# Expert gathers with an index bound: rows of empty slots are no longer fetched

## The reference, cut to what matters

```python
def moe_ffn(h, w_rg, b_rg, w_re, b_re, w_g, w_u, w_d):
    ...
    e_idx = grp[:, None] * EXPERTS_PER_GROUP + e_loc
    ...
    xb = h_pad[slot_tok].reshape(n_blk, EXPERT_BLOCK, D)
    ...
    def run(args):
        xe, e = args
        return (jax.nn.silu(xe @ w_g[e]) * (xe @ w_u[e])) @ w_d[e]
    ...
    return jax.ops.segment_sum(y_assign, tok_sorted, num_segments=N).astype(h.dtype)
```

## Time and profile before

| | us |
|---|---|
| median of 3 runs | 993.66 |
| the profiled execution | 996.17 |
| its span, first to last instruction | 994.3 |
| TensorE busy in the span | 948.4 |
| VectorE busy | 550.7 |
| ScalarE busy | 190.1 |
| GpSimd busy | 59.1 |

### The profile page before, as it was taken

How to read it: one execution, slowest core, us unless ns; L and a number is a source line. 1 busy time by engine, 2 the same in 40 slices (tenths; PEclk the granted TensorE clock), 3 DMA queues, 4 the chain that set the end, 5 groups by cost and what they waited for, 6 DMA issues and landing times.

```text
span 994.3 us, 11254 instructions
## 1 busy us (share of the span) xinstructions
PE 948.4 (95%) x4417; PEld 468.3 (47%) x4417; DVE 550.7 (55%) x1074; ACT 190.1 (19%) x419; POOL 59.1 (6%) x70
## 2 busy tenths in 40 slices
PE   5999998999999999889999999999999999998997
PEld 2575666877654445643333333333333333333443
DVE  2205440446876412474777777777776667677133
ACT  4011121002755210131111111111111111112201
POOL 3010023000000000010000000000000000000000
PEclk9999999999999999899999999999999999999899
DMA  9590353250001791559999999999999999999111
GB/s 283 171 304 16 75 156 104 86 189 22 2 1 34 196 412 45 234 218 415 420 421 420 418 420 421 419 419 419 421 419 420 421 418 420 420 421 406 69 42 48
DMA packets 72954, 265.01 MB, mean 267 GB/s; under 512 B 11096, under 2 KB 35044, under 8 KB 47908
## 3 DMA queue, kind: packets, MB, share of 16 engines
q1 hardware_dynamic: 68368, 251.32, 64.5%
q0 software_dynamic: 4080, 12.85, 3.7%
q10 hardware_dynamic: 452, 0.11, 0.1%
HBM read 253.24 MB, written 13.08 MB: 268 GB/s over the span
## 4 chain that ended last, share of the span: by engine, by line
PE 75%; SPq 12%; DMA 6%; DVE 4%; ACT 1%; issue 1%; ACTq 0%; DVEq 0%
PE ps L1002 67%; SPq L348 12%; DMA w<-in_w_exp_up 3%; DMA w<-in_w_exp_down 3%; PE ps L1361 2%; PE ps L1020 1%; PE ps L1618 1%; PE ps L1655 1%; PE ps L1102 1%; PE ps L1103 1%; DVE h L2505 0%; DMA gmix<-in_norm_mix 0%; ACT probs L825 0%; PE ps L1364 0%; PE ps L1170 0%
## 5 line engine op out<-in xcount | busy, mean ns | idle before, releaser
L1002 PE MATMUL ps<-w,xe 128*64 128x512 f32 x1024 | 233.6, 598 | 11.6 <-DMA w<-in_w_exp_up 10.6
L2463 DVE TENSOR_TENSOR h<-h,ps 128x1024 f32<-128x1024 f32 (+1 forms) x150 | 177.4, 1216 | 31.4 <-PE ps L1002 29.4
L1002 PEld LDWEIGHTS ps<-w,xe 128*64 128x64 f32 x1024 | 70.0, 136 | 145.9 <-issue 139.1
L1002 PE MATMUL ps<-w,hT 128*64 128x512 f32 x512 | 116.9, 598 | 0.7 <-DVE hT L2440 0.5
L1002 PE MATMUL ps<-xT,wring 128*128 128x272 f32 x384 | 101.7, 403 | 2.8 <-issue 2.8
L1002 PE MATMUL ps<-yk,ST 128*128 128x512 f32 (+1 forms) x320 | 95.3, 413 | 0.5 <-DVE yk L2454 0.5
L1002 PE MATMUL ps<-wring,xT 128*32 128x128 f32 (+2 forms) x368 | 80.8, 413 | 1.4 <-DVE xT L391 1.4
L1002 PEld LDWEIGHTS ps<-xT,wring 128*128 128x128 f32 x384 | 68.5, 190 | 28.9 <-issue 16.2
L956 ACT ACTIVATE sg<-ps 64x256 f32<-64x256 f32 x64 | 24.1, 377 | 266.5 <-PE ps L1002 266.1
L674 POOL DMA_INDIRECT xg<-hn_rows,sidx x32 | 30.2, 944 | 667.1 <-PE ps L1618 388.3
L1002 PEld LDWEIGHTS ps<-w,hT 128*64 128x64 f32 x512 | 34.4, 136 | 66.6 <-issue 65.8
(11 more groups left out here) (341 smaller groups left out, 867.4 us busy)
## 6 DMA issues: line engine op xcount, KB each, us to landing
w<-in_w_exp_gate SPq DMA_DIRECT2D x64, 1024.0 KB, 26.2
w<-in_w_exp_up SPq DMA_DIRECT2D x64, 1024.0 KB, 27.4
w<-in_w_exp_down SPq DMA_DIRECT2D x64, 1024.0 KB, 27.4
wring<-in_w_in SPq DMA_DIRECT2D x12, 512.0 KB, 6.2
wpg<-in_w_ple_gate SPq DMA_DIRECT2D x2, 2048.0 KB, 13.5
biaslines<-blrow SPq DMA_DIRECT2D x1, 2560.0 KB, 10.6
h<-in_x_prompt SPq DMA_DIRECT2D x4, 512.0 KB, 12.3
wring<-in_w_in SPq DMA_DIRECT2D x2, 1024.0 KB, 10.9
```

Source lines behind the costliest of these rows:

```text
L1002: return nc.tensor.matmul(out, l, r, start=start, stop=stop, skip_group_check=skip)
L2463: TTn(h[0:r, t, :], h[0:r, t, :], both(4 + 2 * (t % 2), r), ALU.add).then_inc(S["hadd"], 1)
```

## The change

Token numbers in `tokf` are lowered by 4096 (`NOROW`), and `2 * 4096` is added when `sidx` is made. A filled slot has the index it had. An empty slot sums to 0 and gets index 8192 or 8193. The gather carries the bound `2 * N - 1 = 1087` and doesn't treat an index over it as an error: such a row is to be left out, and the partition keeps what it held.

```diff
+NOROW = 4096
...
                 pool.indirect_dma_start(out=xg[:, two(J), :], out_offset=None, in_=hn_d.rearrange("n (k d) -> (n k) d", k=2),
-                                        in_offset=bass.IndirectOffsetOnAxis(ap=at, axis=0)).then_inc(S[f"gath{two(J)}"], 16)
+                                        in_offset=bass.IndirectOffsetOnAxis(ap=at, axis=0), bounds_check=2 * N - 1,
+                                        oob_is_err=False).then_inc(S[f"gath{two(J)}"], 16)
...
                     for k in range(2):
-                        V.tensor_copy(tokf[:, k, :], tok[:])
+                        V.tensor_scalar(tokf[:, k, :], tok[:], float(-NOROW), None, ALU.add)
...
-            TS(sidx[0:SLOTS, :], ps[0:SLOTS, 6, 0:JOBS], 2.0, None, ALU.mult)
-            TS(sidx[SLOTS:P, :], ps[0:SLOTS, 6, 0:JOBS], 2.0, 1.0, ALU.mult, ALU.add).then_inc(S["ix_ok"], 1)
+
+            TS(sidx[0:SLOTS, :], ps[0:SLOTS, 6, 0:JOBS], 2.0, 2.0 * NOROW, ALU.mult, ALU.add)
+            TS(sidx[SLOTS:P, :], ps[0:SLOTS, 6, 0:JOBS], 2.0, 2.0 * NOROW + 1.0, ALU.mult, ALU.add).then_inc(S["ix_ok"], 1)
```

## The result

The changed kernel took 985.12 us (median of 4 runs, 984.98 to 987.06), the kernel before 992.95 us beside it (median of 4, 992.14 to 994.12): ratio 0.9923, 95% interval 0.9908 to 0.9938, so 6.2 to 9.1 us less. Forecast was 5.0 us less and 988.7 us; the time lies in the range and the sign is right, the gain is half as large again.

What follows compares the result with a forecast made beforehand. DMA was taken to bound the expert stage, PE waiting for weights after 720 us. The only nonzero term, 5.0 us less for left-out gather rows, took the median 993.66 us to 988.7 us; range 984.0 to 994.7 us.

Steps and rivals of the forecast that it cites:

- The bound: Expert stage: DMA full from about 446 us, PE waiting for weights only after 720 us, at most 11.0 us to gain.
- The steps that cost nothing: VectorE additions, the first two gathers and POOL's index check: each counted as 0 us.
- The layout: Later 30 gathers: each engine writes 4 adjacent partitions and the 4 lying 32 higher; gain 5.0 us within 0 to 9.1.
- the term of the sum: Empty half rows left out of the later 30 gathers, priced at 5.0 us less, between 0 and 9.1 us.
- Rival A: Later gathers: relief is even over the engines, gain 8.7 to 9.1 us, time 984.7 us; chance 0.22.
- rival B: Later gathers: nothing gained, by 8 adjacent slots on the busiest engine or left-out rows costing their packet; 993.7 us, chance 0.22.
- Rival C: First gather: the index check on POOL holds it up, 4 us slower at 997.7 us; chance 0.08.
- Rival D: Expert stage: all of PE's 11.0 us of waits vanish, packets also being cheaper; 982.7 us, chance 0.06.
- the relief that counts is that of the busiest engine: Later gathers: weights land only when all 16 engines finish, so the least relieved counts: 61 half rows at 0.082, 5.0 us.
- what would show it: Signs for the profile after: q0 about 4.2 MB and fewer packets, PE's waits near 6 us, DMA share below 1.01.

Runs made afterwards that it cites:

- e3: Changed kernel with every index over the bound, so no gather fetches a row (timing only); ratio 0.9855 to the kernel before, stage 451.7 us.
- e11: Changed kernel with the bound kept but the indexes of the kernel before, so every row is fetched; ratio 0.9996, stage 464.4 us.
- e12: Changed kernel with the gathers of jobs 0 and 1 fetching all their rows; one run, 990.45 us beside 994.81 us before, stage 457.0 us.
- e1: Changed kernel leaving out slots 32 to 63 in every gather, filled or not (timing only); ratio 0.9886 to the kernel before, stage 455.0 us.
- e2: Changed kernel leaving out slots 4 to 7, 12 to 15 and so on, filled or not (timing only); ratio 0.9997, stage 463.9 us.
- e5: Changed kernel leaving out slots 2, 3, 6, 7 and so on (timing only); one run, 986.27 us beside 995.12 us before, stage 454.9 us.
- e6: Changed kernel fetching only slots 0 to 3 and 32 to 35 (timing only); one run, 991.50 us beside 995.12 us before, stage 460.5 us.
- e8: Changed kernel fetching only slots 28 to 31 and 60 to 63 (timing only); one run, 991.49 us beside 995.12 us before, stage 460.9 us.
- e4: Changed kernel with slots dealt over the engine groups by two constant tables, result kept; 989.42 us beside 995.32 us, ratio 0.9933, stage 456.6 us.
- e9: The changed kernel itself, run and profiled again on another chip; 987.99 us beside 994.81 us before, ratio 0.9925, stage 457.1 us.
- e7: Changed kernel fetching only slots 8 to 11 and 40 to 43 (timing only); one run, 994.05 us beside 995.12 us before, stage 463.4 us.

## Why the prediction was right, and where its size was off

**The bound** was read rightly. PE leads with 14.31 us for a job until the lead of the weight buffers is used up, and bytes left out earlier are paid back only after that. e3 shows that the early ones count: 9 gathers are issued after 720 us (POOL's x9 in the earlier trace rows), which in full cost 9 x 0.66 = 5.9 us, and e3 saved 12.4. The chain now changes at 766 us (forecast about 820), PE's waits are 4.4 us (forecast 6.0).

**The steps that cost nothing** do. The two additions on `tokf` take 168 ns each as the casts of the earlier trace rows did, L2397 and L2398 0.20 us each as in the earlier trace rows. POOL's 53 ns and the first two gathers are settled by e11 and e12.

**The layout** was the point on which the term of the sum hung, between 0 and 9.1 us; e1, e2, e5 and the late increments of e6 to e8 show it as forecast. Rival A fell by e2, although its time, 984.7 us, was nearest to the 985.1 us measured: a right number is not a right mechanism. Of rival B, the form in which a left-out row costs its packet is half there: the number of packets stays, the bytes don't, and 0.06 us of 0.66 us remain for a gather. Rival C fell by e11. Rival D's ceiling is real but not reached; e3 is where it lies.

**The step that failed** is "the relief that counts is that of the busiest engine", which priced the term at 61 x 0.082 = 5.0 us. The runs gave 7.0 us in the stage. The price of a half row was a bit too high (0.076 by e1), so the step by itself would have given only 4.6 us. The main thing is that the fullest group, that of slots 0 to 3, was not the one that set the landings: it has 3.6 us of slack (e6), so it would have allowed 61 x 0.076 + 3.6 = 8.2 us, and the group of slots 8 to 11 would have allowed 100 x 0.076 + 0.7 = 8.3 us. The sum for each engine is its relief plus its slack, and the smallest of these decides. Slots 4 to 7 have the next smallest relief, 87: 6.6 us, which with 0.4 us of slack would be the 7.0 measured. The remaining groups are rid of 111 or more, 8.4 us. The group of slots 4 to 7 was not looked at alone, so which one decides is argued, not shown. What the trace does show is that it is a single engine: in a load of the changed kernel that ends at 877.74 us the last increment comes 0.9 us after the one before it, where in the kernel before the last eight come within 0.7 us (887.95 to 888.58 us).

The rule is good to about half a microsecond. For e4 it gives 100 x 0.076 + 0.4 = 8.0 us for slots 4 to 7, and 7.5 were measured. It also finds an engine with next to no slack: e2 gained 0.2 us with the groups of slots 0, 8, 16 and 24 full, of which the first two have 3.6 and 0.7 us of slack, so one of the other two has at most 0.2. In the changed kernel these are rid of 113 and 139 half rows and don't bind.

I had taken 16 engines with a share of 1.01 for 16 engines of one pace; the share is a mean over them and can't say that.

Three signs in "what would show it" were wrong too. The packets of q0 should have become fewer; there are 80 to a gather as before, while the bytes came out as forecast (4.24 MB for 30 gathers in e9, 4.2 forecast). L674 should have stayed near 944 ns; it takes 997, because the check costs POOL something. And the mean DMA share should have fallen, as light engines idle. It stayed 1.01. The likely reason is the queue: weights land 24.6 to 26.9 us after their issue (medians of gate, down and up), so a light engine has that much to go on with, and a difference of at most 149 - 61 = 88 half rows is 7 us. From 720 to 890 us the rate did fall in e6 and e7, to 415 and 411 GB/s, where the difference is 240 half rows, 18 us:

```profile
720.00:890.00 170.00, 162.41 (x724) 61.96 (x722) 119.83 (x147) 22.48 (x46) 8.98 (x9) 1.00 1.01 415
```

```profile
720.00:890.00 170.00, 160.37 (x713) 61.51 (x710) 117.53 (x145) 21.40 (x45) 9.00 (x9) 1.00 1.00 411
```

In e6 all of the fall comes late (419 GB/s from 770 to 860 us, 396 from 860 to 890), probably because the 14 light engines are then done with their weights. e2 has the same difference and kept 419 GB/s from 720 to 890 us.

The difference between the stage's 7.0 us and the 7.8 us of the medians is within the interval.

## What to carry to other kernels

Where a stage is bound by DMA, bytes that a gather need not fetch are worth their time even if PE is busy without a gap for the first half of the stage: look for the point at which the lead runs out. But count them for each DMA engine, not in total: the same 3.94 MB were worth 9.1 us or 0.2 us by the partitions they would have gone to. And when the length of a profile and the medians disagree, measure a stage between two instructions that bracket it; here the changed kernel's stage repeated within 0.1 us in two profiles where whole executions scattered by several.

One condition comes with the change. `xg` is not cleared, so the empty slots hold what lay there before, and `combine` multiplies their results by 0. That is 0 only as long as they are finite.

## What the runs showed that I had not expected

- The DMA engines don't have equal room in this kernel: with all other rows gone, one group with its full rows let the stage end 3.6 us earlier than the 464.1 us of before, another only 0.7 us. The runs don't show why.
- Rows over the bound don't change the number of packets, 80 for a gather in every run that was counted, and cost next to nothing: a gather without a single row takes 0.06 us of each engine.
- The bound lengthens the gather's instruction from 944 to 997 ns or a little more (1000 in e2 and e7) whether any row is left out or not.
- The part of the kernel ahead of the change scatters by 5 us between profiled executions of the same program (first gather at 435.6 and 440.5 us).
